# Seven block products for a feed-forward up projection, with the activations kept in device memory

## What is computed

```python
h2 = rmsnorm(x, w['norm2_g'])
up = h2 @ w['ffn_up']                                   # 1024 -> 2 * 2816, gate and value
up_ext = jnp.concatenate([ffn_hist, up], axis=1)
g_ff, u_ff = jnp.split(causal_dwconv(up_ext, ...), 2, axis=-1)   # three taps along the tokens
x = x + (jax.nn.silu(g_ff) * u_ff) @ w['ffn_down']      # 2816 -> 1024
# then a final RMSNorm; the last two rows of up_ext are an output too
```

## Time and profile before

| | |
|---|---|
| time, median of 3 runs | 1912.9 us (1912.85 to 1915.51) |
| profiled execution | 1913.81 us, its span 1912.0 us |
| TensorE busy | 96% of the span |
| VectorE, GpSimd, ScalarE busy | 47%, 30%, 21% |
| DMA | 112.93 MB, mean 59 GB/s |
| feed-forward stage | from about 1109 us to the end |

### The profile page before, as it was taken

How to read it: one execution, slowest core, us unless ns; L and a number is a source line. 1 busy time by engine, 2 the same in 40 slices (tenths; PEclk the granted TensorE clock), 3 DMA queues, 4 the chain that set the end, 5 groups by cost and what they waited for, 6 DMA issues and landing times.

```text
span 1912.0 us, 29333 instructions
## 1 busy us (share of the span) xinstructions
PE 1829.1 (96%) x11392; PEld 1759.0 (92%) x11392; DVE 898.8 (47%) x1324; ACT 392.1 (21%) x574; POOL 577.8 (30%) x532
## 2 busy tenths in 40 slices
PE   6979899999999999999999989999999999999998
PEld 6978887789899888999999989999999999999997
DVE  5773323426533343222243465554555555554554
ACT  5201123423311122111120042111111111111113
POOL 2413211022223323333332314324323423422430
PEclk9989999999999999999999999999999999999999
DMA  4220311022121221222223311111111111111102
GB/s 139 56 56 22 88 50 46 12 84 59 47 69 57 79 76 56 84 75 64 83 82 83 101 32 56 45 34 55 44 33 55 44 33 55 47 38 47 55 23 100
DMA packets 157665, 112.93 MB, mean 59 GB/s; under 512 B 10844, under 2 KB 148377, under 8 KB 157588
## 3 DMA queue, kind: packets, MB, share of 16 engines
q1 hardware_dynamic: 155284, 103.68, 19.0%
q10 hardware_dynamic: 2304, 8.18, 1.1%
HBM read 95.35 MB, written 16.45 MB: 58 GB/s over the span
## 4 chain that ended last, share of the span: by engine, by line
PE 89%; DVE 6%; ACT 2%; issue 1%; POOL 1%; DMA 1%; SPq 0%; DVEq 0%; ACTq 0%; POOLq 0%
PE ps L1992 18%; PE ps L1998 17%; PE ps L1995 17%; PE ps L2188 9%; PE ps L2455 5%; PE pt L2559 3%; PE pt L2561 3%; PE pt L2560 3%; PE ps L2170 2%; PE ps L2233 1%; PE pt L2220 1%; DVE h_lo L1879 1%; PE pt L2597 1%; PE pt L2599 1%; PE pt L2598 1%
## 5 line engine op out<-in xcount | busy, mean ns | idle before, releaser
L1992 PE MATMUL ps<-h_hi,w_hi 128*128 128x352 f32 x2112 | 463.8, 328 | 18.2 <-DVE h_lo L1879 6.0
L1998 PE MATMUL ps<-h_hi,w_lo 128*128 128x352 f32 x2112 | 456.6, 324 | 0.0
L1995 PE MATMUL ps<-h_lo,w_hi 128*128 128x352 f32 x2112 | 455.8, 324 | 0.0
L1992 PEld LDWEIGHTS ps<-h_hi,w_hi 128*128 128x128 f32 x2112 | 358.5, 190 | 22.8 <-issue 13.3
L951 POOL TENSOR_TENSOR mark<-eps 128x1 f32<-128x1 f32 x159 | 44.9, 282 | 1087.7 <-PE ps L1998 544.0
L1998 PEld LDWEIGHTS ps<-h_hi,w_lo 128*128 128x128 f32 x2112 | 363.1, 189 | 0.0
L1995 PEld LDWEIGHTS ps<-h_lo,w_hi 128*128 128x128 f32 x2112 | 360.0, 189 | 0.0
L958 POOL TENSOR_TENSOR w_lo<-w_raw,w_hi 128x1024 fp32r<-128x1024 f32 x126 | 331.8, 2633 | 10.1
L1923 DVE TENSOR_TENSOR y_all<-y_all,pt 128x352 f32<-128x352 f32 x234 | 122.0, 521 | 115.1 <-PE pt L2561 89.8
L1903 DVE SCALAR_TENSOR_TENSOR cv<-ext,pv,cv 128x1072 f32<-128x1072 f32 x88 | 143.5, 1631 | 11.0 <-DVE cv L1903 0.2
L2559 PE MATMUL pt<-act_hi,w_hi 128*128 128x352 f32 x432 | 140.4, 325 | 4.2 <-DVE y_all L1923 4.2
(11 more groups left out here) (386 smaller groups left out, 2176.7 us busy)
## 6 DMA issues: line engine op xcount, KB each, us to landing
w_raw<-in_w_in SPq DMA_DIRECT2D x52, 512.0 KB, 4.3
w_raw<-in_ffn_up SPq DMA_DIRECT2D x44, 512.0 KB, 3.8
w_raw<-in_ffn_down SPq DMA_DIRECT2D x22, 512.0 KB, 3.5
gate_raw<-y_all ACTq DMA_DIRECT2D x15, 528.0 KB, 2.7
cst<-gate_raw SPq DMA_DIRECT2D x15, 528.0 KB, 3.6
x_tok<-in_x_prompt SPq DMA_DIRECT2D x8, 512.0 KB, 6.2
bw_raw<-in_w_branch SPq DMA_DIRECT2D x32, 128.0 KB, 3.5
w_raw<-in_w_out SPq DMA_DIRECT2D x8, 512.0 KB, 4.9
```

Of the source, the lines that this page charges most:

```text
L1992: mm(dst[:, c, 0:CH], f_hi[n][:, k, :], h_hi[:, k, tok], start=k == 0, stop=False)
L1995: mm(dst[:, c, 0:CH], f_hi[n][:, k, :], h_lo[:, k, tok], start=False, stop=False)
L1998: last = mm(dst[:, c, 0:CH], f_lo[n][:, k, :], h_hi[:, k, tok], start=False, stop=k == KD - 1)
```

## The change

The first two of the 22 blocks are computed as before. For the other 20 the gate and value products of one block are taken together as a product of a 2 x 2 matrix of weight blocks (features in two halves of four row blocks, gate and value) with a 2 x 2 matrix of inputs (the same halves, tokens in two halves HT = 528), in Winograd's form with seven block products in place of eight. Each is 24 matmuls (4 row blocks x 3 parts x 2 chunks of HC = 264). Its inputs are sums and differences: of the input, made once at the start of the stage (`combos_sum`, `combos_lower`, `combos_upper`, in `tw` and `y_all_r`), and of the weights, made for each block by GpSimd (`weight_sum`, four of 512 wide), then rounded by ScalarE (`weight_upper`, seven) and split by GpSimd (`weight_lower`, seven). Two products are added to another one in PSUM (S2 on A11, S4 on S1); ScalarE saves banks 0 and 1 to `mid` after A11 and after S2 (`snapshot`); VectorE reads the other banks five times and adds (`put_together`), and then multiplies with the norm (`normed`), now from SBUF.

The activations go to device memory (`act_kept`), as does the residual (`x1_kept`). The down projection is a stage behind the up projection: three thirds of the tokens by two halves of the outputs, each pass 11 groups of two weight row blocks, four output blocks accumulated over all 11 in PSUM, one addition of the residual at the end. The groups' weights are rounded by ScalarE and split by GpSimd; the activations are loaded and split again. Output tiles of a third are made while the next third is multiplied. The hardware loops over the blocks are gone; all is unrolled. Gone with them are the functions that made the loops (`load_ffn`, `split_ffn`, `up`, `down`, `ffn_front`, `ffn_upper`, `ffn_tokens`, `ffn_sums`), whose removed lines are left out below. The core of the diff:

```diff
+    x1_kept = nc.dram_tensor("x1_kept", (KD, P, T), F32, kind="Internal").ap()
+    act_kept = nc.dram_tensor("act_kept", (NFF, P, T), F32, kind="Internal").ap()
...
+    tw = sb(s46, "tw", [P, 4, KH, HT], F32R)
...
+    H_OPS = [lambda k: (h_hi[:, k, 0:HT], h_lo[:, k, 0:HT]),
+             lambda k: (h_hi[:, KH + k, 0:HT], h_lo[:, KH + k, 0:HT]),
+             lambda k: (x1_r(k, 0), x1_r(k, 1)),
+             lambda k: (tw[:, 2, k, :], tw[:, 3, k, :]),
+             lambda k: (tw[:, 0, k, :], tw[:, 1, k, :]),
+             lambda k: (x1_r(KH + k, 0), x1_r(KH + k, 1)),
+             lambda k: (h_hi[:, KH + k, HT:T], h_lo[:, KH + k, HT:T])]
+    NW = len(H_OPS)
+    BANKS = (0, 2, 0, 4, 6, 2, 6)
+    OPENS = (True, True, False, True, True, True, False)
+    A11, A12, S2, S3, S1, A22, S4 = range(NW)
...
+    w_sum = {S1: 0, S2: 1, S3: 2, S4: 3}
...
+    NG = NFF // 2
+    PASSES = [(c, mh) for c in range(3) for mh in range(2)]
+    ND = NG * len(PASSES)
...
+    R11, R3, R22, R21, R12 = range(1, 6)
...
+        def keep_x1(k):
+            row = bass.ds(at(k), 1)
+            sp.wait_ge(wo_read, k + 1)
+            sp.dma_start(x1_kept[row].rearrange("o p t -> p (o t)"),
+                         x1[:, row, :].rearrange("p o n -> p (o n)")).then_inc(x1_sent, 16)
...
+        def load_pair(e):
+            sp.wait_ge(w_split, W6 + 2 * N_PLAIN if e == N_PLAIN else weights_split(e - 1, A22))
+            for n in range(2):
+                sp.dma_start(w_raw[n][:, :, :], w_up[:, :, n * FF + e * P:n * FF + (e + 1) * P]).then_inc(ld_f[n], 16)
...
+        load_plain(0)
+        load_plain(1)
+        for k in range(KD - 2, KD):
+            keep_x1(k)
+        load_plain(2)
+        load_plain(3)
+        keep_act(0)
+        load_pair(N_PLAIN)
+        for e in range(N_PLAIN, LAST):
+            load_pair(e + 1)
+            keep_act(e - 1)
...
+        def weight_sum(j):
+            raw_g, raw_u = w_raw
+            g1, g2, u1, u2 = raw_g[:, 0:KH, :], raw_g[:, KH:KD, :], raw_u[:, 0:KH, :], raw_u[:, KH:KD, :]
+            first, second, op = {S1: (u1, u2, ALU.add), S2: (w_source(S1), g1, ALU.subtract),
+                                 S3: (g1, u1, ALU.subtract), S4: (g2, w_source(S2), ALU.subtract)}[j]
+            od.run(g.tensor_tensor(w_source(j), first, second, op), w_summed)
+        def weight_lower(e, j):
+            gp.wait_ge(s_hi_done, S_HI + NW * (e - N_PLAIN) + j + 1)
+            hi, lo = W_SLOTS[j]
+            od.run(g.tensor_tensor(lo, w_source(j), hi.bitcast(F32), ALU.subtract), w_split)
...
+        split_plain(2)
+        combos_lower(0)
+        gp.wait_ge(up_full, 2)
+        split_plain(3)
+        for k in range(1, KH):
+            combos_lower(k)
+        for e in range(N_PLAIN, NFF):
+            for n in range(2):
+                gp.wait_ge(ld_f[n], 16 * (e + 1))
+            if e == N_PLAIN:
+                weight_lower(e, A11)
+                weight_lower(e, A12)
+                gp.wait_ge(up_full, 2 * N_PLAIN)
+            for j in (S1, S2, S3, S4):
+                weight_sum(j)
+            for j in range(2 if e == N_PLAIN else 0, NW):
+                weight_lower(e, j)
+        for q in range(ND):
+            gp.wait_ge(d_hi_done, q + 1)
+            od.run(g.tensor_tensor(pair_rows(d_lo[q % 3][:, :, :]), d_raw[q % 4],
+                                   pair_rows(d_hi[q % 3][:, :, :]).bitcast(F32), ALU.subtract), w_split)
...
+        def weight_upper(e, j):
+            if j in w_sum:
+                act.wait_ge(w_summed, W_SUMMED + 4 * (e - N_PLAIN) + w_sum[j] + 1)
+            else:
+                act.wait_ge(ld_f[0 if j != A22 else 1], 16 * (e + 1))
+            if e > N_PLAIN:
+                act.wait_ge(up_full, multiplied(e - 1, j))
+            elif j >= 2:
+                act.wait_ge(up_full, 2 * N_PLAIN)
+            od.run(sc.activation(W_SLOTS[j][0], w_source(j), ACT.Copy), s_hi_done)
+        def snapshot(e, n):
+            act.wait_ge(up_full, multiplied(e, A11 if n == 0 else S2))
+            if e > N_PLAIN:
+                act.wait_ge(up_read, read_back(e - 1, R11 if n == 0 else R12))
+            else:
+                act.wait_ge(h2_split, 2 * KD)
+                act.wait_ge(t_rest, 2 * KH)
+            od.run(sc.activation(in_half(mid[:, n, :]), side(A11), ACT.Copy), snap_done)
...
+        for k in (0, KH):
+            scaled(k)
+        plain_front(0, 0)
+        combos_upper(0)
+        for k in (1, KH + 1):
+            scaled(k)
+        plain_front(0, 1)
+        silu(0, 1)
+        combos_upper(1)
+        for k in (2, KH + 2, 3, KH + 3):
+            scaled(k)
+        combos_upper(2)
+        plain_front(1, 0)
+        combos_upper(3)
+        weight_upper(N_PLAIN, A11)
+        weight_upper(N_PLAIN, A12)
+        plain_front(1, 1)
+        silu(1, 3)
+        for j in range(S2, S4):
+            weight_upper(N_PLAIN, j)
+        for e in range(N_PLAIN, NFF):
+            more = e < LAST
+            weight_upper(e, S4)
+            if e > N_PLAIN:
+                gate_front(e - 1)
+            snapshot(e, 0)
+            if more:
+                weight_upper(e + 1, A11)
+                weight_upper(e + 1, A12)
+            if e > N_PLAIN:
+                silu(e - 1, 2 * N_PLAIN + by_g(e - 1))
+            snapshot(e, 1)
+            if more:
+                for j in range(S2, S4):
+                    weight_upper(e + 1, j)
+            else:
+                down_upper(0)
+                act_upper(0)
+                down_upper(1)
+            value_front(e)
+        act_upper(1)
...
+        def combos_sum(k):
+            dve.wait_ge(y_scaled, Y_SCALED + 2 * (k + 1))
+            if k > 0:
+                dve.wait_ge(t_rest, 2 * k)
+            b11, b12, b21, b22 = (quarter(x1, row, second) for row in (k, KH + k) for second in range(2))
+            od.run(v.tensor_tensor(mid[:, 0, :], b12, b11, ALU.subtract))
+            od.run(v.tensor_tensor(mid[:, 1, :], b22, b12, ALU.subtract))
+            od.run(v.tensor_tensor(mid[:, 2, :], b22, mid[:, 0, :], ALU.subtract))
+            od.run(v.tensor_tensor(mid[:, 3, :], mid[:, 2, :], b21, ALU.subtract), t_sum)
+        def combos_lower(k):
+            dve.wait_ge(t_hi_done, T_HI + 4 * k + 4)
+            for n, row in ((2, k), (3, KH + k)):
+                od.run(v.tensor_tensor(x1_r(row, 1), mid[:, n, :], x1_r(row, 0).bitcast(F32), ALU.subtract), h2_split)
...
+        def put_together(e, n):
+            j, k, second = {R11: (A12, 0, 0), R3: (S3, None, 0), R22: (S1, 1, 1), R21: (A22, 1, 0), R12: (S4, 0, 1)}[n]
+            dve.wait_ge(up_full, multiplied(e, j))
+            if n in (R11, R3):
+                dve.wait_ge(snap_done, SNAP + 2 * (e - N_PLAIN) + n)
+            dst = in_half(mid[:, 2, :] if k is None else cv[k][:, second * HT:(second + 1) * HT])
+            kept = in_half(mid[:, {R11: 0, R3: 1, R22: 2, R21: 2, R12: 1}[n], :])
+            if n == R21:
+                od.run(v.tensor_tensor(dst, kept, side(j), ALU.subtract), up_read)
+            else:
+                od.run(v.tensor_tensor(dst, side(j), kept, ALU.add), up_read)
...
+        dve.wait_ge(h2_split, KD)
+        plain_tokens(0, 0)
+        ffn_conv(0, 0, 1)
+        combos_sum(0)
+        combos_lower(0)
+        plain_tokens(0, 1)
+        ffn_conv(0, 1, 2)
+        combos_sum(1)
+        ffn_product(0)
+        combos_lower(1)
+        combos_sum(2)
+        combos_lower(2)
+        plain_tokens(1, 0)
+        ffn_conv(1, 0, 3)
+        combos_sum(3)
+        combos_lower(3)
+        plain_tokens(1, 1)
+        ffn_conv(1, 1, 4)
+        ffn_product(1)
+        for e in range(N_PLAIN, NFF):
+            if e > N_PLAIN:
+                put_together(e - 1, R12)
+                normed(e - 1, 0)
+                ffn_conv(e - 1, 1, 2 * N_PLAIN + by_u(e - 1))
+                ffn_conv(e - 1, 0, 2 * N_PLAIN + by_g(e - 1))
+                ffn_product(e - 1)
+            put_together(e, R11)
+            put_together(e, R3)
+            put_together(e, R22)
+            if e == LAST:
+                act_lower(0)
+            put_together(e, R21)
+            normed(e, 1)
+        put_together(LAST, R12)
+        normed(LAST, 0)
+        act_lower(1)
+        ffn_conv(LAST, 1, 2 * N_PLAIN + by_u(LAST))
+        act_lower(2)
...
+        def pair_ready(e, j):
+            if j == A11:
+                if e == N_PLAIN:
+                    pe.wait_ge(up_read, 2 * N_PLAIN - 1)
+                else:
+                    pe.wait_ge(snap_done, SNAP + 2 * (e - N_PLAIN))
+            elif j == A12:
+                pe.wait_ge(up_read, 2 * N_PLAIN if e == N_PLAIN else read_back(e - 1, R21))
+            elif j == S2:
+                pe.wait_ge(snap_done, SNAP + 2 * (e - N_PLAIN) + 1)
+                if e == N_PLAIN:
+                    pe.wait_ge(h2_split, 2 * KD)
+            elif j == S3:
+                if e == N_PLAIN:
+                    pe.wait_ge(t_rest, 2 * KH)
+                else:
```

(36 more changed lines are left out.)

649 lines of the change are left out of this document (360 added, 289 removed).

## The result

The changed kernel takes 1936.7 us (median of 4 runs, 1934.1 to 1938.4) against 1912.9: ratio 1.012, 95% interval 1.010 to 1.014. It is slower by 1.2%. The forecast, 1916, was "no change"; the measured time is 21 us above it. It lies within the range of 8 in 10 (1887 to 1943), but above the forecast's own range (1903 to 1930) and inside that of rival (c), 1930 to 1965. The profiled execution took 1934.1, span 1932.3.

The account below looks back on a forecast made before the run. TensorE's matmuls were taken to bound the kernel. Terms -49 + 25 + 23.4 + 11.5 + 3 - 10 + 1.7 - 3.8 = +1.8 on 1913.8 gave 1915.6, stated as 1916 us; own range 1903 to 1930, 8 in 10 1887 to 1943.

Parts of the forecast that it names:

- rival (c): Steady pairs: GpSimd's chain of split, load, sums and subtractions is longest, pair 23.7 us; 1945 (1930 to 1965), chance 0.2.
- 1, 2. Matmuls and down projection: Up products: 264-column matmuls take 0.1235 us, a pair 20.75 against 23.2; down projection keeps its 255 us, zero change.
- the term -49: Up products: us saved by fewer, narrower matmuls over 20 pairs, 20 x (20.75 - 23.2).
- 3. Turn-taking at SBUF: Steady pairs: GpSimd and two-SBUF-input VectorE operations exclude each other; one turn of both about 2.2 us, PSUM reads unaffected.
- 4. The steady pair: Steady pairs: collisions delay A22, so a pair takes 22.2 us, 1.45 over TensorE's own; bounds 21.2 and 23.3.
- the term +25: Steady pairs: us lost over 17 pairs by TensorE's wait before A22.
- The circle: Steady pairs: A22 waits for VectorE's read R11, behind two convolutions, silu and product; period 22.2 us.
- 5. The start: Before the first pair TensorE stops, +23.4 us (17 to 28); blocks 2 and 3 take 53.0 against 41.5, +11.5.
- 6. Edges: Down stage entry +3 us, old stage's waits -10, 16 more transposes +1.7, tail -3.8.
- (b): Steady pairs: TensorE sets the pace, collisions fit into the slack before A22; 1886 us (1876 to 1903), chance 0.26.
- (d): Up products: the narrow matmul isn't shorter in proportion, 0.135 us; 1928 (1920 to 1936), chance 0.07.

Follow-up runs that it names:

- snap_first: The changed kernel with ScalarE's snapshot of A11 put ahead of the gate's first tap; 1952.9 us.
- vec_lower: The changed kernel with the subtractions for A11's and A12's weights moved from GpSimd to VectorE, as one of 1024; 1948.0 us.

## Why the forecast was off, step by step

**1, 2. Matmuls and down projection** were right. The pitch is 0.122 (0.1235 said) and a pair without waits 20.5 (20.75), so the term -49 measures -54. The down stage with its transposes takes 268.3 from first to last matmul, of which 265.3 was in the sum: three waits of 1.9, 1.9 and 3.3. The run with 20 plain blocks puts the stage level with the old one.

**3. Turn-taking at SBUF** was right in kind: the 32-wide scaling at 1.17, the 1024-wide product at 2.33, reads of PSUM at 0.71 throughout. The rows listed for VectorE add up to 13.6, not 14.7; nothing else rests on it. The Trainium skill (SBUF — State Buffer, "SBUF: two separate sides") says that whichever starts first has the pair for the whole instruction; the trace agrees, 1.17 for 0.19.

**4. The steady pair** is the step that failed, in its size: 22.93 for 22.2, 389.5 for 377.4 over 17 pairs, +12.1. Against TensorE's own 20.5 a pair pays 2.4, not 1.45, and the term +25 measures +41. The circle was the right one, and the wait is where it was put, before A22, released by VectorE's read. The size missed because I placed GpSimd wrongly in time. I let A22's split end 0.4 us after A11's start; it ends 4.5 after (1451.52). Of the ten GpSimd operations from the load to that split four take 1.76 to 2.17 for 1.29. So the load lands at 10.7, not at 5.7, and the sums fall behind the convolution instead of on it: that saves most of the 1.6 I charged there, but the two scalings, which I had nearly free, cost 0.41 and 0.98 each. In all, VectorE's operations in the circle exceed their undisturbed lengths by 5.7 us a pair. That the phase of the collisions could be wrong the prediction had said itself. The 0.85 in front of S2, also not forecast, costs nothing (`snap_first`).

**5. The start**: the stop is 23.0 (23.4 said), ended by GpSimd's split of A11's weights, as said. Blocks 2 and 3 took 57.4 for 53.0: behind the stop the granted clock was 0.73 over 1184 to 1200, and A11 and S2 of block 2 took 5.4 and 4.2 for 2.9, which I hadn't counted. With the plain blocks' combinations interleaved and spread the stop went from 23.0 to 7.8 and 0: it was work on VectorE's queue, which in part waited for ScalarE.

**6. Edges**: the end takes 12.1, for 10.7 said and 14.5 before; the first part of the kernel was 2.3 shorter in this execution. Together: 1913.8 of span expected + 12.1 + 4.4 + 3.0 (down stage) + 1.4 (end) + 0.6 (last pair) - 2.3 - 0.4 = 1932.6, against 1932.3.

**The rivals.** (b) would have needed every wait before A22 to vanish: pairs of 20.4 to 20.5 occur, but never more than two in a row. (c) has the measured time in its range, and GpSimd's circle is closed: in the steady pairs it is idle only while the load that its own split asked for is under way. But its mark, a wait in front of A11 released by GpSimd, is not there; with two operations fewer on GpSimd (`vec_lower`) no pair fell below 22.65; and bringing its load forward made the kernel 66 us slower. Free of collisions GpSimd's circle would be some 20 us (ten operations of 1.3 with their gaps, and 6.2 from the split to the first sum) and VectorE's 17; it is their collisions that lengthen both. The four runs fit this account, but no run has the pairs without collisions. (d) is out by the pitch.

## What to carry to other kernels

When two engines take turns at a resource, add the lengths only as a first bound; what counts is which operations of one fall on the critical ones of the other, and a wait (here for a load) may be what keeps them apart, so removing work or starting it earlier can cost more than it saves. Placing the off-path engine's work with a gate behind the critical stretch helped here once that engine had less to do, and not before. Test each edit by the period of a steady turn, not by the busy time. Before a wait is taken away, look where its time goes: two short waits of TensorE cost no more than themselves, and the same time in one piece was followed by half clock in 10 of 17 pairs.
